# FoX attention: both parts of the values in one stationary operand, one channel summed on GpSimd, each load issued by itself

## The reference, cut to what matters

```python
logits = jnp.einsum('bqhd,bkhd->bhqk', qblk, k) * scale
logits = logits + cblk.swapaxes(1, 2)[..., None] - ck_t[:, :, None, :]   # cumulative log-forget of query and key
logits = jnp.where(k_pos[None, :] <= pblk[:, None], logits, -jnp.inf)
probs = jax.nn.softmax(logits, axis=-1)
out = jnp.einsum('bqhk,bkhd->bqhd', probs, v)
```

## Time and profile before

| | us |
|---|---|
| median of 3 executions | 1909.41 |
| lowest and highest | 1909.07, 1911.21 |
| the profiled execution | 1911.22 |
| span of the profiled execution | 1909.2 |
| projections | 0 to 1069.5 |
| attention of the prompt, heads 0 to 6 | 1069.5 to 1434.7 |
| head 7 | 1434.7 to 1476.0 |
| sample attention, merge, output norm | 1476.0 to 1909.2 |

### The profile page before, as it was taken

One profiled execution on the slowest core, in us unless ns is written; L12 is line 12 of the kernel. 1 busy time (PEld: TensorE's weight loads), 2 busy tenths in 40 slices (PEclk: granted clock), 3 DMA queues, 4 the chain that ended last, 5 costly groups with the idle time before them and its releaser, 6 DMA issues.

```text
span 1909.2 us, 28724 instructions
## 1 busy us (share of the span) xinstructions
PE 1863.5 (98%) x10604; PEld 1724.8 (90%) x10604; DVE 1293.6 (68%) x2255; ACT 853.7 (45%) x1594; POOL 185.8 (10%) x153
## 2 busy tenths in 40 slices
PE   7999999999999999999999999999999899999998
PEld 6999999999999999999999787788778799998885
DVE  8878787944445365444656688888896734457887
ACT  5545546633344443433323577777778600111100
...
GB/s 225 261 330 284 309 319 286 321 230 323 265 295 315 282 295 223 297 233 326 269 295 243 200 32 122 123 134 134 134 106 144 243 370 218 245 184 159 140 146 72
DMA packets 272782, 435.99 MB, mean 228 GB/s; under 512 B 63252, under 2 KB 139188, under 8 KB 268508
## 3 DMA queue, kind: packets, MB, share of 16 engines
...
## 4 chain that ended last, share of the span: by engine, by line
PE 83%; DVE 8%; issue 2%; DMA 2%; SPq 2%; ACT 2%; POOLq 0%; POOL 0%; DVEq 0%; ACTq 0%
PE fr_b L639 4%; PE fr_b L640 4%; PE fr_b L641 4%; PE fr_c L639 4%; PE fr_c L640 4%; PE fr_c L641 4%; PE fr_a L640 4%; PE fr_a L641 4%; PE fr_a L639 4%; PE ln_b L2543 3%; PE ln_b L2545 3%; PE ln_b L2544 3%; PE at_o L1687 3%; PE at_m L1703 3%; PE at_s L1670 3%; PE at_s L1671 3%
## 5 line engine op out<-in xcount | busy, mean ns | idle before, releaser
L815 ACT ACTIVATE fr_wq<-fr_raw 128x512 fp32r<-128x512 f32 x288 | 178.1, 627 | 207.1 <-PE fr_d L641 137.4
L1780 DVE TENSOR_TENSOR at_p_lo<-at_s,at_p_hi 128x512 fp32r<-128x512 f32 (+1 forms) x320 | 191.9, 603 | 42.8 <-ACT at_s L1750 41.3
L1749 ACT ACTIVATE at_p_hi<-at_s 128x512 fp32r<-128x512 f32 (+1 forms) x320 | 169.7, 530 | 84.0 <-PE at_s L1671 49.3
L1105 DVE TENSOR_TENSOR fr_wq<-fr_raw,fr_wq 128x512 fp32r<-128x512 f32 x288 | 192.2, 683 | 9.1 <-ACT fr_wq L815 5.8
L639 PE MATMUL fr_b<-fr_xh,fr_wq 128*128 128x348 f32 x568 | 186.2, 328 | 9.6 <-DVE fr_wq L1105 5.7
L639 PE MATMUL fr_a<-fr_xh,fr_wq 128*128 128x348 f32 x568 | 183.6, 323 | 0.6 <-ACT fr_p L898 0.6
L639 PE MATMUL fr_c<-fr_xh,fr_wq 128*128 128x348 f32 x568 | 183.6, 323 | 0.3 <-DMA fr_wq<-w_mixed 0.3
L641 PE MATMUL fr_b<-fr_xh,fr_wq 128*128 128x348 f32 x568 | 183.9, 324 | 0.0
L640 PE MATMUL fr_b<-fr_xl,fr_wq 128*128 128x348 f32 x568 | 183.8, 324 | 0.0
L640 PE MATMUL fr_a<-fr_xl,fr_wq 128*128 128x348 f32 x568 | 183.1, 322 | 0.0
L641 PE MATMUL fr_a<-fr_xh,fr_wq 128*128 128x348 f32 x568 | 182.5, 321 | 0.0
...
## 6 DMA issues: line engine op xcount, KB each, us to landing
...
```

What stands on the lines that cost most here:

```text
L815: act.activation(wh[:, idx], operand(i, idx), ACT.Copy).then_inc(w_hi[idx], 1)
L1105: dve.tensor_tensor(wl[:, idx], operand(i, idx), wh[:, idx].bitcast(F32), ALU.subtract).then_inc(w_lo[idx], 1)
L1749: act.activation(p_hi[:, r, cols], s_bank[r][:, cols], ACT.Exp, scale=SCALE)
L1780: dve.tensor_tensor(p_lo[:, r, cols], s_bank[r][:, cols], p_hi[:, r, cols].bitcast(F32), ALU.subtract)\
```

## The change

- v_hi and v_lo of a head now stand side by side in one stationary operand, `v_both`: columns 0 to 63 are v_hi, columns 64 to 127 v_lo. One matmul with p_hi and one with p_lo give all four partial products; those with the two parts of one channel stand 64 rows of o apart. Column 64, the low part of channel 0, is overwritten by ones, and row 64 of o is the row sum as before.
- The low part of channel 0 is kept in `v_first`, whose other columns are zero. In 28 of a head's 40 steps its product with p_hi is the third matmul. In the other 12 steps (kb odd and below 4q: "pooled" steps 5, 7, 13 to 19, 25 to 35) GpSimd multiplies p_hi by the 128 keys' values of this channel and adds the terms up in `acc`, 12 multiplications and 9 additions a head; one matmul per query block 1 to 3 (`close`) adds the sum over the partitions to o. Before ACT writes a buffer of p_hi that a pooled step read, it waits for GpSimd's multiplication.
- ACT copies rows 64 to 127 of o into `part` (`copy_part`, after its step e + 5, where e is the last step of the query block), and DVE's take, now after its step e + 4, becomes part x lanes + o, where lanes is 0 for the row sum and 1 for the others.
- The reciprocals are made for each query block by themselves, in steps 13 (block 3 of the head before), 16, 23 and 33, each with its own transfers. GpSimd's and ACT's further work on y is placed anew by hand.
- Loads of the next head are issued one by one between these transfers: its values first, at the head's start, and `max_rows` after the store of the reciprocals of block 2. In head 7, the four loads of the sample's keys take the places of `load_main`.
- The lead's low values are loaded within the projections and not at their end. GpSimd moves the low part of channel 0 and sets the ones, once a head.

The diff, cut to its core:

```diff
-
-            def load_lead_low():
-                for idx in (0, 2, 5):
-                    sp.wait_ge(w_lo[idx], NSETS - 1)
-                load_lead_v(1, s["vl"])
...
                 if i == 2 * PER + 19:
                     load_lead_v(0, s["vh"])
-                if i == NSETS - 1:
-                    load_lead_low()
+                    load_lead_v(1, s["vl"])
...
-            pool.memset(v0[0][:, :, HD:P].bitcast(F32), 1.0).then_inc(lead_ones, 1)
...
-            pool.memset(v0[1][:, :, HD:P].bitcast(F32), 0.0).then_inc(lead_ones, 1)
-            pool.wait_ge(lead_ones, 5)
+            pool.memset(v0[1][:, :, 1:P].bitcast(F32), 0.0).then_inc(lead_ones, 1)
+            pool.wait_ge(lead_ones, 4)
...
-        v_hi, v_lo = (main[:, :, 2 + x].rearrange("p a (b c) -> p a b c", c=P) for x in range(2))
+        v_both, v_first = (main[:, :, 2 + x].rearrange("p a (b c) -> p a b c", c=P) for x in range(2))
...
-        INVERT = 9
-        FINISH = {20 + 4 * q + x + x // 2: (q, x) for x in range(3) for q in range(NQ)}
-        FINISH_LOW = {st + 5: q for st, (q, x) in FINISH.items() if x == 0}
+        INVERT = {16: (0, 0), 23: (0, 1), 33: (0, 2), 13: (1, 3)}
+        SCALE_AT = {22: (0, 0), 38: (0, 1), 0: (1, 2), 20: (1, 3)}
+        GATE_AT = {23: (0, 0), 39: (0, 1), 1: (1, 2), 21: (1, 3)}
+        UPPER_AT = {30: (0, 0), 4: (1, 1), 6: (1, 2), 28: (1, 3)}
+        LOWER_AT = {37: (0, 0), 9: (1, 1), 10: (1, 2), 36: (1, 3)}
+        V_AT = 11
+        PART_AT = {(e + 5) % NS: (0 if e + 5 < NS else 1, q) for q, e in enumerate(ends)}
+        TAKE_AT = {(e + 4) % NS: (0 if e + 4 < NS else 1, q) for q, e in enumerate(ends)}
         TURN = 32
...
+        def pooled(st):
+            q, kb = steps[st]
+            return kb < 4 * q and kb % 2 == 1
...
         def sum_store(sp, h, q):
-            sp.wait_ge(o_read, NQ * h + q + 3)
-            sp.dma_start(s["sums"][h:h + 1, q * QW:(q + 1) * QW], y[HD:HD + 1, h % 2, q * QW:(q + 1) * QW])\
+            sp.wait_ge(part_done, NQ * h + q + 1)
...
+        def sums_load(sp, h, q):
+            sp.wait_ge(sum_out, 16 * (NQ * h + q) + 16)
+            sp.dma_start(sums[:, 4 * q:4 * q + 4], s["sums"][h:h + 1, q * QW:(q + 1) * QW].rearrange("a (p b) -> (a p) b", p=P))\
+              .then_inc(sums_in[q], 16)
+
+        def rcp_store(sp, h, q):
+            sp.wait_ge(rcp_done, NQ * h + q + 1)
+            sp.dma_start(s["rcps"][h:h + 1, q * QW:(q + 1) * QW].rearrange("a (p b) -> (a p) b", p=P), rcp[:, 4 * q:4 * q + 4])\
+              .then_inc(rcp_out, 16)
+
+        def rcp_load(sp, h, q):
+            sp.wait_ge(rcp_out, 16 * (NQ * h + q) + 16)
+            if h:
+                sp.wait_ge(y_scaled, NQ * (h - 1) + q + 1)
+            sp.dma_start(rcp_all[:, q * QW:(q + 1) * QW], s["rcps"][h:h + 1, q * QW:(q + 1) * QW].broadcast_to([HD, QW]))\
+              .then_inc(rcp_in[q], 16)
...
+            def load_ahead(h, n):
+                if h + 1 < H:
+                    load_main(h + 1, n)
+                else:
+                    sam.key_load(sp, n)
+
+            def load_values(h):
+                rows, b = slice(h * HD, (h + 1) * HD), h % 2
+                if h > 1:
+                    sp.wait_ge(closed, 3 * (h - 1))
+                for x, of in enumerate((s["vh"], s["vl"])):
+                    sp.dma_start(v_both[:, b, :, x * HD:(x + 1) * HD].bitcast(F32),
+                                 of[0:SEQ, rows].rearrange("(b p) c -> p b c", p=P)).then_inc(v_in[b], 16)
+
+            def load_gate(h):
+                if h > 1:
+                    sp.wait_ge(y_gated, NQ * (h - 1))
+                sp.dma_start(zb[:, h % 2], s["zb"][h * HD:(h + 1) * HD, 0:SEQ]).then_inc(zb_in[h % 2], 16)
...
+                if h + 1 < H:
+                    load_values(h + 1)
+                if h == 1:
+                    sam.early_loads(sp)
                 if h:
                     sum_store(sp, h - 1, 3)
-                    sums_load(sp, h - 1)
-                    rcp_store(sp, h - 1)
-                    rcp_load(sp, h - 1)
-                sp.dma_start(zb[:, h % 2], s["zb"][h * HD:(h + 1) * HD, 0:SEQ]).then_inc(zb_in[h % 2], 16)
-                if h + 1 < H:
-                    if h:
-                        sp.wait_ge(pv_done, NS * h + RING)
-                    load_main(h + 1)
-                if h + 2 < H:
-                    if h == 0:
-                        sp.wait_ge(ones_set, 2)
-                    load_max(h + 2)
-                if h == 1:
-                    sam.early_loads(sp)
-                if h == H - 1:
-                    sam.key_loads(sp)
+                    sums_load(sp, h - 1, 3)
+                load_ahead(h, 0)
                 sum_store(sp, h, 0)
-                sum_store(sp, h, 1)
-                if h:
-                    y_store(sp, h - 1, 0)
-                sum_store(sp, h, 2)
                 if h:
                     y_store(sp, h - 1, 1)
+                sums_load(sp, h, 0)
+                load_ahead(h, 1)
+                if h:
+                    y_store(sp, h - 1, 2)
+                    rcp_store(sp, h - 1, 3)
+                    rcp_load(sp, h - 1, 3)
+                load_ahead(h, 2)
+                rcp_store(sp, h, 0)
+                sum_store(sp, h, 1)
+                rcp_load(sp, h, 0)
+                sums_load(sp, h, 1)
+                load_gate(h)
+                load_ahead(h, 3)
+                rcp_store(sp, h, 1)
+                load_max(h + 2, 0)
+                rcp_load(sp, h, 1)
+                load_max(h + 2, 1)
+                sum_store(sp, h, 2)
+                load_max(h + 2, 2)
+                sums_load(sp, h, 2)
+                rcp_store(sp, h, 2)
                 if h + 1 < H:
                     max_rows(sp, h + 1)
+                rcp_load(sp, h, 2)
                 if h:
-                    y_store(sp, h - 1, 2)
                     y_store(sp, h - 1, 3)
+                if h < H - 1:
+                    y_store(sp, h, 0)
 
...
                 o = o_bank[q % 2][:, cols]
-                pe.matmul(o, v_hi[:, b, kb, :], p_hi[:, r, cols], start=(kb == 0), stop=False)
-                pe.matmul(o, v_hi[:, b, kb, :], p_lo[:, r, cols], start=False, stop=False)
-                pe.matmul(o, v_lo[:, b, kb, :], p_hi[:, r, cols], start=False, stop=(kb == 4 * q + 3))\
-                  .then_inc(pv_done, 1)
+                pe.matmul(o, v_both[:, b, kb, :], p_hi[:, r, cols], start=(kb == 0), stop=False)
+                last = pe.matmul(o, v_both[:, b, kb, :], p_lo[:, r, cols], start=False, stop=False)
+                if not pooled(st):
+                    last = pe.matmul(o, v_first[:, b, kb, :], p_hi[:, r, cols], start=False, stop=(q == 0 and kb == 3))
+                last.then_inc(pv_done, 1)
+
+            def close(h, q):
+                if h == 0 and q == 1:
+                    pe.wait_ge(first_row_set, 2)
+                pe.wait_ge(acc_done, added_through(h, q))
+                pe.matmul(o_bank[q % 2][:, :], first_row[:, :], acc[:, :], start=False, stop=True).then_inc(closed, 1)
...
                     values(h, b, st)
+                    if h and st == 0:
+                        close(h - 1, NQ - 1)
+                    if st - 1 in ends[1:-1]:
+                        close(h, ends.index(st - 1))
...
+                before = (h, st - RING) if st >= RING else (h - 1, st - RING + NS)
+                if before[0] >= 0 and pooled(before[1]):
+                    act.wait_ge(acc_scaled, pooled_through(*before))
...
+            def copy_part(h, q):
+                n = NQ * h + q
+                if q:
+                    act.wait_ge(closed, 3 * h + q)
+                else:
+                    act.wait_ge(pv_done, NS * h + ends[q] + 1 + RING)
+                if n >= 2 * NQ:
+                    act.wait_ge(sum_out, 16 * (n - 2 * NQ + 1))
+                    act.wait_ge(o_read, n - 2 * NQ + 3)
+                act.activation(part[HD:2 * HD, n % (2 * NQ), :], o_bank[q % 2][HD:2 * HD, :], ACT.Copy).then_inc(part_done, 1)
...
-                dve.wait_ge(pv_done, NS * h + ends[q] + 1 + RING)
+                dve.wait_ge(part_done, NQ * h + q + 1)
                 if h > 1:
                     dve.wait_ge(yl_done, NQ * (h - 1))
-                dve.tensor_copy(y[:, b, q * QW:(q + 1) * QW], o_bank[q % 2][0:HD + 1, :]).then_inc(o_read, 1)
+                o = o_bank[q % 2]
+                dve.scalar_tensor_tensor(out=y[0:HD, b, q * QW:(q + 1) * QW], in0=part[HD:2 * HD, (NQ * h + q) % (2 * NQ), :], scalar=lanes[HD:2 * HD, :],
+                                         in1=o[0:HD, :], op0=ALU.mult, op1=ALU.add).then_inc(o_read, 1)
...
-                if b:
-                    take(h, b, NQ - 1)
-
+                    job = at_step(TAKE_AT, h, st)
+                    if job:
+                        take(job[0], job[0] % 2, job[1])
+                    if at_step(INVERT, h, st):
+                        invert(dve, *at_step(INVERT, h, st))
+
+            def free_first_channel(h):
```

(24 more changed lines are left out.)

142 lines of the change are left out of this document (82 added, 60 removed).

## The result

| | before | after |
|---|---|---|
| median, us | 1909.97 (1909.07 to 1911.21, 4 runs) | 1939.88 (1937.44 to 1941.37, 4 runs) |
| ratio to before, 95% interval | | 1.0156 (1.0142 to 1.0170) |
| profiled execution, its span | 1911.22, 1909.2 | 1941.37, 1939.6 |
| forecast | | 1897.2 (1888 to 1909) |

The kernel became 30 us slower; the forecast was 12 us faster. The two profiled spans differ by 30.4 us, and the starts of heads (PE's first value matmul of step 0) say where: the attention starts 1.8 earlier (1068.00 for 1069.79), head 0 takes 0.9 more, head 1 6.3, heads 2 to 6 3.3 each (16.5 in all), head 7 8.2 (to the start of its last value matmul), and all that follows 0.3.

What follows compares the result with a forecast made beforehand. DVE, closely followed by PE, was taken to pace steps 0 to 29, and a chain of waits to lengthen steps 30 to 39. Terms -1.2 - 10.5 - 1.3 + 0.8 = -12.2 us gave 1899.0 profiled, 1897.2 median (1888 to 1909).

Steps and rivals of the forecast that it cites:

- The bound: Steps 0 to 29 of a head, 40.98 us: PE has 2.6 us of slack, DVE 1.6, with DVE in front.
- The waits that were to go: Steps 0 to 29: three waits of DVE for PE, about steps 9 and 21, would vanish, giving 0.8 us a head.
- The take: DVE, attention: the take becomes an addition of two sources but keeps the copy's duration of 0.69 us.
- The tail: Steps 30 to 39: fewer matmuls and one ACT upper moved out of the chain gain 1.2 us a head (0.35 to 1.75).
- The wait for the maxima's rows: Head's end: transfers queued behind the third reciprocals' store make PE wait 0 to 0.5 us, taken as 0.1.
- GpSimd at nothing: Attention heads: GpSimd's work, 38.1 us of 51.94 with 0.9 us per multiplication, was costed at nothing.
- Does GpSimd slow DVE? ... no: Attention: DVE's subtraction takes 680 ns with GpSimd idle or working, so GpSimd was taken not to slow DVE.
- Junction: Attention's start: issuing the lead's low values earlier removes PE's wait for the maxima's rows, gaining 1.2 us (0 to 1.4).
- The end of attention: After the last head: the last take follows a closing matmul and ACT's copy, losing 0.8 us (0 to 1.5).
- Head 7 and the loads one by one: Head 7 gains 1.3 us (0 to 2.1); sums' chains land 3 to 5 us early, so nothing is charged.
- GpSimd as the bound: Rival, chance 0.10: GpSimd's 33 operations fill a head at a mean of 1.57 us; about +25 us, so 1934.
- reciprocals late: Rival, chance 0.08: chains of sums reach DVE 1 us late at three places in seven heads, giving 1918 us.

Runs made afterwards that it cites:

- act_take: The kernel before, with the take made by ACT, as a copy of 65 rows, instead of DVE: 1906.45 us, ratio 0.9980.
- nopool: The changed kernel with no pooled step, so the third matmul is back in all 40 steps and the closing matmuls are gone: 1923.75 us, ratio 1.0079.
- nopool_copy: The changed kernel with no pooled step and with a plain copy of 64 rows as DVE's take: 1917.14 us, ratio 1.0040.
- take_early: The changed kernel with the take of a head's last query block after DVE's step 2 of the next head instead of step 3: 1942.40 us, ratio 1.0177.
- half: The changed kernel with GpSimd's multiplications and additions for channel 0 over 256 of the 512 columns: 1928.77 us, ratio 1.0100.
- pool9: The changed kernel with 9 pooled steps a head instead of 12; steps 31, 33 and 35 keep their third matmul on PE: 1936.89 us, ratio 1.0148.
- defer7: The changed kernel with head 7's reciprocals of blocks 1 and 2 made behind DVE's last subtraction, their transfers moved behind too: 1945.06 us, ratio 1.0189.

## Why the prediction was wrong, point by point

The sum failed at three of its terms: GpSimd was costed at nothing and cost 16.1 us net, the take was to keep its duration and cost 6.6, and nothing was charged for chains of sums behind other loads, which shows in heads 1 and 7. The gains beside them were over-sized, at the pace of steps 0 to 29 and in the tail.

**The bound.** "So PE has 2.6 us of slack there and DVE 1.6" was wrong for PE where it counts: with 2.1 us taken from DVE, steps 0 to 29 fell only from 40.98 to 40.46 (act_take). By columns PE would be at 38.4; that it can't come down to them because its pieces wait for banks is argued, not tested. The two engines were within half a microsecond of each other; "DVE in front" was right. That fits the 1.4 us of matmuls removed there, which were worth nothing (43.13 against nopool's 43.06).

**The waits that were to go.** "Follow pooled steps and go: 0.8" failed. DVE's waits of 0.27 and 0.35 about step 21 are 0.26 and 0.33 after the change; only the 0.23 about step 9 shrank, to 0.09. In nopool, with the third matmul back in all steps, the three are 0.25, 0.34 and 0.09: pooled steps have no part in them. That they come from the order in which PE meets the short diagonal steps is likely, and not tested.

**The take.** "I keep its duration" was the dearest step for DVE. The operation came out at 0.745, but costs 0.89 from start to start where the copy cost 0.61: 1.2 us a head (nopool to nopool_copy), 6.6 us in all. I compared durations in a list of overlapping instructions. PE's wait of 1.1 us for the take at step 4 was not foreseen either, though moving the take (take_early) didn't shorten a head while GpSimd set its length.

**The tail.** "Gain 0.23 + 0.61 + (0.47 - 0.1) = 1.2" was over-sized: with GpSimd in time it is 0.37 (10.92 to 10.55, half), of which 0.12 come without any pooled step. The wait for the maxima's rows, bounded at 0 to 0.5, is not there: PE's first scores of a head start 0.23 to 0.46 after the matmul ahead of them.

**GpSimd at nothing** failed at two places. Its price: 1566 ns for the multiplication is outside of both bounds (0.48 and 1.3 us). The Trainium skill has one-input operations of GpSimd "roughly line-rate" ("GPSIMD Engine Reference", section 4.1, Engine selection); the trace disagrees for this one, which is slower than the two-input addition at 1284. The criterion failed too: "a mean of 51.94 / 33 = 1.57 us" decides nothing here. The mean was 1.39, below it (350 us of work in 252 operations), and GpSimd was late nevertheless: six of the twelve multiplications and five of the nine additions fall into eleven steps, a pair lasts 3.11 us there with 0.25 between its operations, and the operations ahead of them wait in order, 2.7 us for a load. The condition in the paragraph on GpSimd, a pair against two steps, was the right one; a pair at both upper bounds came to 2.6 there, and I gave it 2.7 us, from steps 0 to 29, where steps 30 to 39 leave 2.2.

**"Does GpSimd slow DVE? ... no"** was too wide: the subtraction, with one source in PSUM, keeps its 680 ns (683 after). Operations of 16 columns on SBUF alone were held until GpSimd's operation ended (1.15 us for 0.175 in pool9, 0.52 for 0.17 in the mean of the kernel before). The Trainium skill, "GPSIMD Engine Reference", section 1 (Specifications), names contention for DVE instructions with two SBUF inputs or in a 2-port perf mode; the trace agrees for pool9's operation, which has two SBUF inputs, and in which mode the other one, with a single input, ran, no row shows.

**Junction:** right; the wait of 1.22 at the first piece is gone, and the attention starts 1.8 us earlier (taken as 1.2; one execution against one, and the variants start between 1067.3 and 1072.0). **The end of attention:** the sample stage's first ACT work starts 2.74 us after the last value matmul where it was 1.40, so 1.3 in place of 0.8. All that follows that matmul is 0.3 longer in the two profiled executions, but it spans 430.6 to 435.9 over the variants (defer7 aside), so this 0.3 says little.

**Head 7 and the loads one by one.** "Nothing is charged" was wrong in heads 1 and 7. The slack of 3 to 5 us was read from a head without other loads. In head 7 the 1 MB loads took it, with GpSimd's work as a second condition; in head 1 the early loads made the gate late, and GpSimd and ACT with it. DVE's 5.0 us of wait then cost 6.8 in steps 24 to 27, since PE's clock fell as well (below).

**The rivals.** GpSimd as the bound (0.10) was nearest in time, 1934, and names the engine of 16 of the 30 us, though by a mean that was not reached; reciprocals late (0.08) is in head 7. No rival had the take's price. The slow cases stood as alternatives, each with a chance of its own, and two of them came true at once, with a third loss beside them. In medians the runs part the loss into 16.1 for GpSimd's work (nopool), 6.6 for the form of the take (nopool_copy) and 8.2 that stay open; the losses of heads 1 and 7 are inside these terms and no further ones.
